# FFN second product of groups 0 to 7 as seven block products (Strassen), in a two-layer decoder trunk on one core

## The chip, the cores and the metric

One core of one Trainium2 chip. The metric is device time in microseconds (us) of one execution. The core has TensorE (PE in the profile, its weight loads PEld), VectorE (DVE), ScalarE (ACT), GpSimd (POOL) and SyncE (SP), which issues most transfers. Each engine takes its instructions in the written order and waits on semaphores.

## The reference, cut to what matters

A stream `x` of 256 tokens by 1024 goes through two layers, each a mixer (attention) and a convolutional FFN, with residual and layer norm behind each. All values are float32. The change is in the FFN:

```
def conv_ffn(x, w_in, conv_w, conv_b, w_out):      # w_in 1024 x 5632, w_out 2816 x 1024
    up, gate = split(x @ w_in, 2)
    up = depthwise causal conv of width 3 over tokens (up) + conv_b
    return (gelu(up) * gate) @ w_out
x = layer_norm(ALPHA * x + conv_ffn(x, ...))
```

## The kernel before

`yoco_trunk` writes out each engine's program by hand. Float32 precision is had with three matmuls: each operand is split into a rounded part (`hi`, by ACT, line 790) and the rest (`lo`, by DVE, line 977, as `raw - hi`), and `product` (lines 1286 to 1290) adds hi*hi, hi*lo and lo*hi into one PSUM bank of 512 columns. Weights come in chunks of 128 x 2048 elements (1 MB) into a ring of three `raw` tiles, and are split into rings of four `w_hi` and `w_lo` tiles.

The FFN works through 11 groups of 256 features. For group i:

- `in_product(i)` (line 1462): 16 products, 48 matmuls, tokens as rows, `up` and `gate` features as columns, for two halves of tokens (`st`). Each half fills one bank; two pairs of banks alternate from group 1 on (`in_banks`).
- `turn_in` (line 1206, DVE) transposes each of the two banks in 32x32 blocks into `turned`; `in_move` (line 586, SP) carries the blocks to `in_moved` (a part of the tile `kT`) with four transfers.
- `taps` (lines 897, 898, ACT), `add_taps` (lines 1226, 1229, DVE), `make_gelu` (line 910, ACT), `make_hidden` (line 1214, DVE), `make_h_hi` (line 918, ACT) and `make_h_lo` (line 1219, DVE) make the hidden features, features on partitions, in a ring of four (`HIDDEN`, held in `oT_hi`, `oT_lo`).
- `out_product` (line 1490): 8 products of 128 x 128 by 128 x 512 for the group (two halves of tokens, two halves of output columns, two halves of features), 24 matmuls, summed over all groups in the four banks `wide`. It follows three groups behind `in_product` (`second_behind`).

So PE does 72 matmuls of 512 columns in a group. POOL does almost nothing in the FFN: six weight half splits (line 731) near the layer norms and small powers (lines 754, 763). On SP's queue a group's turned blocks are moved ahead of the load six chunks later (`MOVE_AHEAD`).

Of the kernel before, what the change touches and what calls it, by code (L numbers as in the profile page):

```python
# [39 lines left out]
HIDDEN = 4  # L40
MOVE_AHEAD = 6
# [261 lines left out]
def yoco_trunk(nc, x, positions, a_w_qkv, a_w_o, w_kv_shared, b_w_q, b_w_o, b_lambda, b_subln_g,  # L303
# [14 lines left out]
    LAYER_CHUNKS = QKV_CHUNKS + WO_CHUNKS + 3 * GROUPS  # L318
# [29 lines left out]
    def second_behind(i):  # L348

        if i == GROUPS - 1:  # L350
            return [GROUPS - 4, GROUPS - 3]
        return [i - 3] if i >= 3 else []

    ffn_order = []
    for i in range(GROUPS):
        ffn_order += [(i, 0), (i, 1)] + [(n, 2) for n in second_behind(i)]
    ffn_order += [(GROUPS - 2, 2), (GROUPS - 1, 2)]

    def ffn_chunk(layer, i, which):

        return layer * LAYER_CHUNKS + QKV_CHUNKS + WO_CHUNKS + ffn_order.index((i, which))

    IN_CHUNKS = {ffn_chunk(layer, i, h) for layer in range(LAYERS) for i in range(GROUPS) for h in range(2)}

    def raw_count(c):

        return sum(32 if n in IN_CHUNKS else 16 for n in range(c % RAW_RING, c + 1, RAW_RING))

    ffn_moves_ahead = {}
    for layer in range(LAYERS):  # L370
        for i in range(GROUPS):
            ffn_moves_ahead[ffn_chunk(layer, i, 1) + MOVE_AHEAD] = (layer, i)
# [33 lines left out]
    with ExitStack() as ctx:  # L406
# [6 lines left out]

        raw = [sb(f"raw{s}", [P, CHUNK]) for s in range(RAW_RING)]
# [5 lines left out]
        qk_rows = sb("qk_rows", [P, 2 * ST * HALF])  # L420
# [3 lines left out]
        v_rows = sb("v_rows", [P, ST, D])  # L424
# [17 lines left out]
        conv = headT[0][:, 0:2, :]  # L442
# [1104 lines left out]
```

## Time and profile before

| | us |
|---|---|
| median of 3 runs | 592.69 |
| lowest, highest | 592.50, 593.11 |
| the profiled execution's own time | 593.44 |
| its span, first to last instruction | 590.9 |
| FFN of layer 0 on PE, about | 113.5 to 294.8 |
| FFN of layer 1 on PE, about | 401 to 582 |

The profile is of one execution, 0.1% above the median. The page's busy time of PE counts matmuls from start to modelled end, which overlap: the time that one adds is the distance between two starts. The time of a DVE, ACT or POOL instruction runs from its start to its end; back to back, DVE's overlap by some hundredths of a microsecond. The granted TensorE clock is 1.00 in the windows of both FFN stages.

### The profile page before, as it was taken

Reading aid. Unit: us, or ns where it says so; the run is one execution under the profiler, and the core shown is the slowest. Engines: PE = TensorE matmul, PEld = TensorE weight load, DVE = VectorE, ACT = ScalarE, POOL = GpSimd, SP = SyncE. Lnnn points to the kernel's source line nnn. Section 1 sums busy time; section 2 is a strip of 40 time slices with the busy share of each in tenths; the row PEclk is TensorE's granted clock in tenths of the full one; section 3 lists DMA queues with packets and bytes.
Section 4 is the critical chain, followed back from the end, with each engine's and each line's share of the span. In section 5 each row is a group of like instructions: output and inputs, shape, how many; then the busy total and the mean of one; then the engine's idle time right before and its main releaser. Section 6 shows DMA issues by size and latency. Waiting matters only on the chain.

```text
span 590.9 us, 7752 instructions
## 1 busy us (share of the span) xinstructions
PE 580.6 (98%) x2720; PEld 473.7 (80%) x2720; DVE 448.5 (76%) x813; ACT 335.3 (57%) x560; POOL 50.9 (9%) x84
## 2 busy tenths in 40 slices
PE   8999999999999999999999999999999999999995
PEld 6887777788888888888888888887888888888884
DVE  4889995886688777667879796778677888766656
ACT  4767584245566656554545678944556574555530
POOL 5300000400000000000120003132000000000003
PEclk9999999999999999999999999999999999999998
DMA  8997876456668798866456955442965889777511
GB/s 298 297 325 232 273 176 214 132 182 207 202 211 262 252 336 259 262 207 219 154 202 192 333 175 174 136 143 72 311 184 181 252 257 334 243 235 246 179 36 71
DMA packets 95665, 127.86 MB, mean 216 GB/s; under 512 B 13404, under 2 KB 73612, under 8 KB 95628
## 3 DMA queue, kind: packets, MB, share of 16 engines
q1 hardware_dynamic: 94188, 123.19, 65.3%
q0 software_dynamic: 1152, 4.19, 2.0%
q8 instruction: 21, 0.34, 0.2%
q14 instruction: 16, 0.13, 0.1%
q10 hardware_dynamic: 288, 0.00, 0.0%
HBM read 108.23 MB, written 1.05 MB: 185 GB/s over the span
## 4 chain that ended last, share of the span: by engine, by line
PE 95%; DVE 3%; DMA 1%; ACT 0%; issue 0%; SPq 0%; DVEq 0%
PE wide L1288 18%; PE wide L1290 17%; PE wide L1289 17%; PE score L1290 6%; PE score L1288 6%; PE score L1289 6%; PE outb L1290 3%; PE turn L1290 3%; PE outb L1288 3%; PE turn L1288 3%; PE outb L1289 3%; PE turn L1289 3%; DMA xs<-in_x 1%; DVE xT L994 1%; PE turn L1387 1%; PE outb L1413 1%
## 5 line engine op out<-in xcount | busy, mean ns | idle before, releaser
L977 DVE TENSOR_TENSOR w_lo<-raw,w_hi 128x2048 fp32r<-128x2048 f32 (+1 forms) x120 | 210.5, 1776 | 60.5 <-ACT w_hi L790 60.3
L790 ACT ACTIVATE w_hi<-raw 128x2048 fp32r<-128x2048 f32 (+1 forms) x126 | 184.2, 1488 | 92.3 <-PE wide L1290 45.5
L1288 PE MATMUL wide<-w_hi,oT_hi 128*128 128x512 f32 x240 | 95.0, 396 | 0.0
L1290 PE MATMUL wide<-w_hi,oT_lo 128*128 128x512 f32 x240 | 93.5, 390 | 0.0
L1289 PE MATMUL wide<-w_lo,oT_hi 128*128 128x512 f32 x240 | 93.5, 390 | 0.0
L1288 PE MATMUL wide<-w_hi,xT 128*128 128x512 f32 x224 | 89.9, 401 | 0.5 <-DVE xT L994 0.3
L1290 PE MATMUL wide<-w_hi,xT 128*128 128x512 f32 x224 | 87.4, 390 | 0.0
L1289 PE MATMUL wide<-w_lo,xT 128*128 128x512 f32 x224 | 87.3, 390 | 0.0
L1288 PE MATMUL score<-w_hi,xT 128*128 128x512 f32 x160 | 62.2, 389 | 0.0
L1289 PE MATMUL score<-w_lo,xT 128*128 128x512 f32 x160 | 62.2, 389 | 0.0
L1290 PE MATMUL score<-w_hi,xT 128*128 128x512 f32 x160 | 62.2, 389 | 0.0
L1290 PEld LDWEIGHTS wide<-w_hi,oT_lo 128*128 128x128 f32 x240 | 45.0, 188 | 9.5
L1288 PEld LDWEIGHTS wide<-w_hi,oT_hi 128*128 128x128 f32 x240 | 45.1, 188 | 9.1 <-issue 0.3
L1289 PEld LDWEIGHTS wide<-w_lo,oT_hi 128*128 128x128 f32 x240 | 45.1, 188 | 8.9
L1288 PEld LDWEIGHTS wide<-w_hi,xT 128*128 128x128 f32 x224 | 42.1, 188 | 11.5 <-issue 2.9
L1290 PEld LDWEIGHTS wide<-w_hi,xT 128*128 128x128 f32 x224 | 42.0, 188 | 9.0
L1289 PEld LDWEIGHTS wide<-w_lo,xT 128*128 128x128 f32 x224 | 42.1, 188 | 7.9
L897 ACT ACTIVATE kT<-kT 128x256 f32<-128x256 f32 x44 | 17.9, 406 | 51.5 <-DMA kT<-turned 51.5
L1226 DVE SCALAR_TENSOR_TENSOR qT<-kT,conv_cols,qT 128x255 f32<-128x255 f32 x44 | 21.1, 480 | 25.1 <-ACT qT L898 25.1
L1289 PEld LDWEIGHTS score<-w_lo,xT 128*128 128x128 f32 x160 | 30.0, 188 | 6.3
L1290 PEld LDWEIGHTS score<-w_hi,xT 128*128 128x128 f32 x160 | 30.0, 188 | 6.3
L1288 PEld LDWEIGHTS score<-w_hi,xT 128*128 128x128 f32 x160 | 30.0, 188 | 6.1
(160 smaller groups left out, 837.9 us busy)
## 6 DMA issues: line engine op xcount, KB each, us to landing
raw<-in_ffn_w_in SPq DMA_DIRECT2D x88, 512.0 KB, 5.4
raw<-in_ffn_w_out SPq DMA_DIRECT2D x22, 1024.0 KB, 7.6
kT<-turned SPq DMA_DIRECT2D x104, 128.0 KB, 2.8
raw<-in_a_w_qkv SPq DMA_DIRECT2D x9, 1024.0 KB, 6.8
raw<-in_w_kv_shared SPq DMA_DIRECT2D x8, 1024.0 KB, 7.0
raw<-in_a_w_o SPq DMA_DIRECT2D x4, 1024.0 KB, 6.2
raw<-in_b_w_q SPq DMA_DIRECT2D x4, 1024.0 KB, 5.1
raw<-in_b_w_o SPq DMA_DIRECT2D x4, 1024.0 KB, 5.2
```

The lines of the kernel that those rows point to most:

```text
L790: ins = nc.scalar.activation(w_hi[c % RING][:, part], raw[c % RAW_RING][:, part], ACT.Copy)
L897: nc.scalar.activation(by_quarters(up[:, tt, :]), carried(tt), ACT.Copy)
L977: ins = nc.vector.tensor_tensor(w_lo[c % RING][:, part], raw[c % RAW_RING][:, part], w_hi[c % RING][:, part].bitcast(F32), ALU.subtract)
L994: nc.vector.tensor_tensor(xT_lo[part], side[f][:, :].rearrange("p (k q) -> p k q", k=4), xT_hi[part].bitcast(F32), ALU.subtract).then_inc( ...
L1226: link(nc.vector.scalar_tensor_tensor(conv[:, tt, 1:SEQ], up[:, tt, 0:SEQ - 1], conv_cols[:, layer, FT + 2 * i + tt:FT + 2 * i + tt + 1], ...
L1288: nc.tensor.matmul(dst, a_hi, b_hi, start=start, stop=False, skip_group_check=True)
L1289: nc.tensor.matmul(dst, a_hi, b_lo, start=False, stop=False, skip_group_check=True)
L1290: return nc.tensor.matmul(dst, a_lo, b_hi, start=False, stop=stop, skip_group_check=True)
L1387: last = nc.tensor.transpose(turn_bank[:, b * P:(b + 1) * P], probs[:, slot, b * P:(b + 1) * P], ident[:, :])
L1413: nc.tensor.matmul(part[h][:, 0:SEQ], v_rows[:, 0, col:col + 64], turned_probs[:, (head + h) % 4, 0:2], start=n == 0, stop=False, skip_gro ...
```

## The change

For groups 0 to 7 (`FOLDED`) the second product, a 2 x 2 by 2 x 2 multiplication of blocks (halves of tokens, of features and of output columns), is done by Strassen's seven products instead of eight. Each is summed over the eight groups in a bank of its own: seven banks, `fold_a` (four) and `fold_b` (three). One bank, `side[3]`, is left for the first product of groups 2 to 9, so each half of `in_half` waits until DVE has transposed the half before it.

Five of the seven take sums of two blocks on each side. The sums of hidden blocks are made by DVE (`combine`), and DVE subtracts for seven `h_lo` blocks instead of four. The sums of weight blocks, five in all, are made by POOL (`fold_weights`) from the raw chunk, and POOL also makes their `lo` parts; ACT makes the `hi` parts (`fold_plain_hi`, `fold_sum_hi`, `fold_b_hi`), and DVE the `lo` part of the two blocks used as they are (`fold_plain_lo`). After the last folded product DVE adds the seven banks into `xs` with 12 instructions (`add_folded`). Group 10 has its first product with features on partitions (`in_features`), 96 matmuls of 256 columns instead of 48 of 512, and needs no transposition or move. Four half splits of the second weights of groups 8 and 9 go from DVE to POOL. Each folded group's second weights are loaded ahead of the move of its turned blocks.

```diff
-HIDDEN = 4
-MOVE_AHEAD = 6
+FOLDED = 8
...
         for i in range(GROUPS):
             loads += [("chunk", in_chunk(layer, i, h)) for h in range(2)]
             if 2 <= i < FOLDED + 2:
                 loads.append(("fold", FOLDED * layer + i - 2))
...
-        in_banks = [side[0:2], side[2:4]]
+        fold_a = ((1, wide[0]), (0, side[0]), (2, side[2]), (3, side[1]))
+        fold_b = ((6, wide[1]), (5, wide[3]), (4, wide[2]))
...
+            def fold_weights(t):
+
+                four = quadrants(t)
+                pool.wait_ge(raw_in[raw_slot("fold", t)], raw_count("fold", t))
+                if t:
+                    pool.wait_ge(sum_lo_done, t)
+                nc.gpsimd.tensor_tensor(fold_sums[0].rearrange("p (t n) -> p t n", t=2), four[:, :, 0, :], four[:, :, 1, :],
+                                        ALU.add).then_inc(sums_a_done, 1)
+                if t:
+                    pool.wait_ge(fold_b_lo_done, t)
+                nc.gpsimd.tensor_tensor(fold_sums[1][:, 0:D].rearrange("p (h n) -> p h n", h=2), four[:, 1, :, :], four[:, 0, :, :],
+                                        ALU.subtract)
+                nc.gpsimd.tensor_tensor(fold_sums[1][:, D:D + HALF], four[:, 0, 0, :], four[:, 1, 1, :],
+                                        ALU.add).then_inc(sums_b_done, 1)
+                pool.wait_ge(sum_hi_done, t + 1)
+                nc.gpsimd.tensor_tensor(fold_lo[0][:, CHUNK // 2:CHUNK], fold_sums[0], fold_hi[0][:, CHUNK // 2:CHUNK].bitcast(F32),
+                                        ALU.subtract).then_inc(sum_lo_done, 1)
+                pool.wait_ge(fold_b_hi_done, t + 1)
+                nc.gpsimd.tensor_tensor(fold_lo[1], fold_sums[1], fold_hi[1].bitcast(F32),
+                                        ALU.subtract).then_inc(fold_b_lo_done, 1)
...
+                def combine(i):
+
+                    dve.wait_ge(hidden_done, 2 * (GROUPS * layer + i) + 2)
+                    sums, tile = h_sums, hidden_tiles
+                    nc.vector.tensor_tensor(sums[:, 0:2, :], tile[:, 0:2, :], tile[:, 2:4, :], ALU.add)
+                    nc.vector.tensor_tensor(sums[:, 2:4, :], tile[:, 1:4:2, :], tile[:, 0:4:2, :], ALU.subtract)
+                    nc.vector.tensor_tensor(sums[:, 4, :], tile[:, 0, :], tile[:, 3, :], ALU.add).then_inc(combined_done, 1)
...
+                    if i > 2 or (i, st) == (2, 1):
+                        pe.wait_ge(in_turned, ST * u + st)
...
+                def in_features(which):
...
+                    for tt in range(2):
+                        into = side[3 - which][:, tt * SEQ:(tt + 1) * SEQ]
+                        for kt in range(KT):
...
+                            last = product(into, w_hi[c % RING][:, col:col + P], w_lo[c % RING][:, col:col + P],
+                                           xT_hi[:, kt, :], xT_lo[:, kt, :], kt == 0, kt == KT - 1)
...
+                def out_folded(j, half):
...
+                    for n, (tile, bank) in enumerate(fold_b if half else fold_a):
+                        if half == 0 and n == 2:
+                            pe.wait_ge(sum_lo_done, t + 1)
+                        cols = slice(n * HALF, (n + 1) * HALF)
+                        last = product(bank[:, :], hT_hi[b][:, tile, :], hT_lo[b][:, tile, :],
+                                       fold_hi[half][:, cols], fold_lo[half][:, cols], j == 0, j == FOLDED - 1)
...
-                for i in range(GROUPS):
-                    in_product(i)
-                    for n in second_behind(i):
...
+                for i in range(MOVES):
+                    for st in range(ST):
+                        in_half(i, st)
+                        if i >= 2:
+                            out_folded(i - 2, st)
+                for which in range(2):
+                    in_features(which)
```

DVE in one middle group of layer 0, before. `qT` holds the convolution, gelu and hidden features, `kT` what came by `in_move`, `oT_lo` the hidden features' `lo` part:

```order
L1206 STREAM_TRANSPOSE turned<-score 128x16x32 [waits in_carried,in_rows_done]
L977 TENSOR_TENSOR w_lo<-raw,w_hi 128x2048 [waits hi_done]
L1206 STREAM_TRANSPOSE turned<-score 128x16x32 [waits chunk_used]
L1219 TENSOR_TENSOR oT_lo<-qT,oT_hi 128x256 [waits hhi_done] x2
L977 TENSOR_TENSOR w_lo<-raw,w_hi 128x2048 [waits hi_done] x2
L1226 SCALAR_TENSOR_TENSOR qT<-kT,conv_cols,qT 128x255 [waits tap_done]
L1229 SCALAR_TENSOR_TENSOR qT<-kT,conv_cols,qT 128x254 [waits dve_step]
```

DVE there now, from the last tap of the group before to the weight splits; ahead of these rows stand one transposition and three more taps. `masked` holds the sums of hidden blocks:

```order
L1390 SCALAR_TENSOR_TENSOR qT<-qT,conv_cols 128x254 [waits dve_step]
L1335 TENSOR_TENSOR qT<-qT,kT 128x256 [waits gelu_done,hhi_done]
L1335 TENSOR_TENSOR qT<-qT,kT 128x256 [waits gelu_done]
L1345 TENSOR_TENSOR masked<-qT 128x256 [waits hidden_done]
L1346 TENSOR_TENSOR masked<-qT 128x256
L1347 TENSOR_TENSOR masked<-qT 128x128
L1354 TENSOR_TENSOR fold_lo_a<-raw,fold_hi_a 128x1024 [waits plain_hi_done]
L1362 TENSOR_TENSOR oT_lo<-masked,oT_hi 128x640 [waits hhi_done]
L1365 TENSOR_TENSOR oT_lo<-qT,oT_hi 128x256 [waits hhi_done]
L1323 STREAM_TRANSPOSE turned<-outb 128x16x32 [waits chunk_used]
L1095 TENSOR_TENSOR w_lo<-raw,w_hi 128x2048 [waits hi_done] x2
```

One full weight split left the group, three sums, a half-size split and a longer `lo` came in, and the second transposition stands behind them.

POOL from the FFN of layer 0 to the mixer of layer 1, before:

```order
L739 DMA norm_rows<-in_ln_b 128x1024
L763 TENSOR_TENSOR std_inv<-var_eps,minus_half 128x1 [waits var_done]
L731 TENSOR_TENSOR w_lo<-raw,w_hi 128x1024 [waits hi_done,norm_x_done] x2
L763 TENSOR_TENSOR std_inv<-var_eps,minus_half 128x1 [waits var_done]
L754 TENSOR_TENSOR rms_inv<-mean_sq,minus_half 128x2 [waits mean_sq_done] x4
```

POOL now, the last of eight folded groups and what follows it (`kT` and `spare` hold the sums of weight blocks):

```order
L796 TENSOR_TENSOR kT<-raw 128x1024 [waits sum_lo_done,raw_in1]
L800 TENSOR_TENSOR spare<-raw 128x1024 [waits fold_b_lo_done]
L802 TENSOR_TENSOR spare<-raw 128x512
L805 TENSOR_TENSOR fold_lo_a<-kT,fold_hi_a 128x1024 [waits sum_hi_done]
L808 TENSOR_TENSOR fold_lo_b<-spare,fold_hi_b 128x1536 [waits fold_b_hi_done]
L779 TENSOR_TENSOR w_lo<-raw,w_hi 128x1024 [waits hi_done] x4
L836 TENSOR_TENSOR std_inv<-var_eps,minus_half 128x1 [waits var_done]
```

The five long instructions at the head of these rows stand eight times in each layer's FFN, where POOL had none.

## Rows read from the trace of the kernel before

**Rows 1.** The page's first part: busy time, share, instructions of each engine.

```profile
PE 580.6 (98%) x2720; PEld 473.7 (80%) x2720; DVE 448.5 (76%) x813; ACT 335.3 (57%) x560; POOL 50.9 (9%) x84
```

**Rows 2.** Waits of PE: engine, line, releaser: us, times, longest.

```profile
PE wide L1309 <- DVE oT_hi L1037: 1.5, 1, 1.5
PE turn L1301 <- DVE xs L1034: 1.0, 2, 0.5
```

**Rows 3.** Timeline of PE, group 1, first product: start us, us, what.

```profile
133.22 0.39 PE L1290 MATMUL score<-w_hi,xT 128*128 128x512 f32 x1
...
133.90 0.39 PE L1290 MATMUL score<-w_hi,xT 128*128 128x512 f32 x1
```

**Rows 4.** Groups by line and shape: busy us, mean ns, idle before.

```profile
L977 DVE TENSOR_TENSOR w_lo<-raw,w_hi 128x2048 fp32r<-128x2048 f32 x63 | 143.3, 2284 | 46.1 <-ACT w_hi L790 45.9
L790 ACT ACTIVATE w_hi<-raw 128x2048 fp32r<-128x2048 f32 x64 | 122.2, 1912 | 67.2 <-PE wide L1290 28.2 <-DMA raw<-in_ffn_w_in 24.4 <-PE outb L1290 8.1
...
L977 DVE TENSOR_TENSOR w_lo<-raw,w_hi 128x1024 fp32r<-128x1024 f32 x57 | 67.2, 1215 | 14.4 <-ACT w_hi L790 14.4
...
L790 ACT ACTIVATE w_hi<-raw 128x1024 fp32r<-128x1024 f32 x62 | 62.0, 1051 | 25.1 <-PE wide L1290 17.3 <-DMA raw<-in_a_w_qkv 7.8
...
L898 ACT ACTIVATE qT<-kT,conv_cols 128x256 f32<-128x256 f32 x44 | 25.8, 587 | 0.0
L1229 DVE SCALAR_TENSOR_TENSOR qT<-kT,conv_cols,qT 128x254 f32<-128x254 f32 x44 | 21.3, 483 | 1.6
...
L1214 DVE TENSOR_TENSOR qT<-qT,kT 128x256 f32<-128x256 f32 x44 | 18.4, 422 | 3.9 <-ACT qT L910 1.7
...
L897 ACT ACTIVATE kT<-kT 128x256 f32<-128x256 f32 x44 | 17.9, 406 | 51.5 <-DMA kT<-turned 51.5
...
L731 POOL TENSOR_TENSOR w_lo<-raw,w_hi 128x1024 fp32r<-128x1024 f32 x6 | 14.4, 2409 | 56.4 <-DVE w_lo L977 51.1 <-DVE xs L1034 5.3
L1206 DVE STREAM_TRANSPOSE turned<-score 128x512 f32<-128x512 f32 x20 | 14.2, 710 | 2.7 <-PE score L1290 2.7
...
L994 DVE TENSOR_TENSOR xT<-score,xT 128x512 fp32r<-128x512 f32 x8 | 5.5, 688 | 7.9 <-ACT xT L800 7.9
...
L769 POOL TENSOR_TENSOR xs<-xs,norm_rows 128x512 f32<-128x512 f32 x2 | 2.5, 1277 | 1.1 <-ACT xs L948 1.1
```

**Rows 5.** Windows: busy time of each engine inside layer 0's FFN.

```profile
core 0: us, PE busy (x) PEld busy (x) DVE busy (x) ACT busy (x) POOL busy (x), PEclk, DMA share, GB/s
125.00:285.00 160.00, 160.00 (x707) 132.48 (x707) 116.58 (x144) 90.20 (x120) 1.13 (x2) 1.00 0.77 246
```

**Rows 6.** Timeline of DVE and POOL where a long DVE instruction runs.

```profile
359.51 1.22 DVE L977 TENSOR_TENSOR w_lo<-raw,w_hi 128x1024 fp32r<-128x1024 f32 x1
359.68 1.61 POOL L754 TENSOR_TENSOR rms_inv<-mean_sq,minus_half 128x2 f32<-128x2 f32 x1 [59.64 <-DVE mean_sq L1165]
```

**Rows 7.** The same two engines, 5 us later, beside a shorter one.

```profile
364.31 0.48 DVE L1181 SCALAR_TENSOR_TENSOR oT_lo<-turn,sub_gain,oT_hi 128x256 fp32r<-128x256 f32 x1
...
364.48 0.69 POOL L754 TENSOR_TENSOR rms_inv<-mean_sq,minus_half 128x2 f32<-128x2 f32 x1 [1.64 <-DVE mean_sq L1165]
```

**Rows 8.** Timeline of POOL while DVE is idle.

```profile
11.49 0.26 POOL L695 TENSOR_SCALAR turns<-turns 128x16 f32<-128x16 f32 x1
```

**Rows 9.** Timeline of POOL, the same operation while DVE splits weights.

```profile
15.40 0.53 POOL L703 TENSOR_SCALAR turns<-turns 128x16 f32<-128x16 f32 x1
```

**Rows 10.** Timeline of DVE: one split where a POOL instruction ends, one elsewhere.

```profile
14.50 0.71 DVE L1043 TENSOR_TENSOR w_lo<-raw,w_hi 128x512 fp32r<-128x512 f32 x1
...
16.34 0.68 DVE L1043 TENSOR_TENSOR w_lo<-raw,w_hi 128x512 fp32r<-128x512 f32 x1
```

**Rows 11.** Timeline of PE: four transpositions of 128 columns, then a product.

```profile
118.21 0.63 PE L1301 MATMUL turn<-ident,xs 128*128 128x128 f32 x4 [0.50 <-DVE xs L1034]
118.59 0.48 PE L1288 MATMUL wide<-w_hi,xT 128*128 128x512 f32 x1
```

**Rows 12.** Timeline of PE: its first six matmuls of 512 columns.

```profile
1.45 2.93 PE L1309 MATMUL wide<-oT_hi 128*128 128x512 f32 x6 [1.45 <-DVE oT_hi L1037]
```

More of the change, by code:

```diff
@@ L325, in yoco_trunk @@
         POOL_SPLITS[2 * layer, 0] = ([(c + 1, 0)], [(c + 1, 1)])
+        POOL_SPLITS[2 * layer, 1] = ([], [(c + 2 * GROUPS + n, half) for n in range(2) for half in range(2)])
         c = (layer + 1) * LAYER_CHUNKS
@@ L328, in yoco_trunk @@
             POOL_SPLITS[2 * layer + 1, 0] = ([], [(c + 1, 1), (c + 2, 0)])
-    POOL_PARTS = [part for n in range(2 * LAYERS) for st in range(ST) for parts in POOL_SPLITS.get((n, st), ([], [])) for part in parts]
+    for n in range(2 * LAYERS):
+        for st in range(ST):
+            for parts in POOL_SPLITS.get((n, st), ([], [])):
+                POOL_PARTS += parts
     POOL_CHUNKS = sorted({c for c, _ in POOL_PARTS})
@@ L938, in _ @@
+                    if 1 <= i <= FOLDED:
+                        fold_b_hi(i - 1)
+                    if i < GROUPS - 1:
+                        split_hi(in_chunk(layer, i, 1) + RING)
+                make_h_hi(GROUPS - 1)
+                for c in (base + LAYER_CHUNKS, base + LAYER_CHUNKS + 1):
+                    for half in range(2):
+                        split_hi(c, half)
                 if layer + 1 < LAYERS:
@@ L1222, in add_taps, with add_folded @@
+                def add_folded(adds):
+                    for st, half, bank, op, after in adds:
+                        part = xs[:, st, half * HALF:(half + 1) * HALF]
+                        if after:
+                            dve.wait_ge(folded_added, 12 * layer + after)
+                        nc.vector.scalar_tensor_tensor(part, part, 1.0 if after else ALPHA, bank[:, :], ALU.mult,
+                                                       op).then_inc(folded_added, 1)
                 def add_taps(i):
@@ L1260, in _ @@
+                    split_lo(in_chunk(layer, i, 0) + RING)
+                    if i < MOVES:
+                        split_lo(in_chunk(layer, i, 1) + RING)
+                    else:
+                        make_h_lo(i)
+                        for half in range(2):
+                            split_lo(base + LAYER_CHUNKS, half)
+                        if layer + 1 < LAYERS:
+                            split_shared_lo()
                     if (layer, i) == (0, 0):
@@ L1266, in _ @@
                 n, c = 2 * layer + 1, base + LAYER_CHUNKS
+                dve.wait_ge(folded_added, 12 * (layer + 1))
                 residual(n, 0, 0)
@@ L1503, in out_product @@
-                    return last
-                for i in range(GROUPS):
-                    in_product(i)
-                    for n in second_behind(i):
-                        for st in range(ST):
-                            for half in range(2):
-                                last = out_product(n, st, half)
-                        last.then_inc(chunk_used, 1)
+                        last = product(wide[2 * st + half][:, :], hT_hi[b][:, at + 2 * tt + st, :], hT_lo[b][:, at + 2 * tt + st, :],
+                                       w_hi[c % RING][:, cols], w_lo[c % RING][:, cols], i == FOLDED and tt == 0,
+                                       i == GROUPS - 1 and tt == 1)
```

391 lines of the change are left out of this document (252 added, 139 removed).

## Prediction, made before the changed kernel was run

> **What bounds the kernel now.** I read the page's first part, then what PE waits for, then its timeline inside the FFN. PE is busy 98% of the span [rows 1], its waits for other engines are five, 3.2 us in sum, the longest two 1.5 and 0.5 [rows 2], and in the FFN the next matmul starts 0.68 us after the third before it, from 133.22 to 133.90 [rows 3]: 0.2267 us for each 512 columns. The busy mean of one (0.39) is no price, since neighbours overlap. So PE bounds both FFN stages, and a group costs 72 x 0.2267 = 16.3 us. In a window of 160 us inside the FFN, DVE is busy 116.6 us, ACT 90, POOL 1.1 [rows 5]. DVE has 27% to spare, and POOL looks free. Whether it is free is the question of this case.
>
> **PE's part.** Each folded group has seven products instead of eight, so three matmuls fewer: 8 groups x 2 layers x 3 = 48, and 48 x 0.2267 = **-10.9 us**. A folded group is 69 x 0.2267 = 15.64 us of PE. Group 10 swaps 48 matmuls of 512 columns for 96 of 256. No row has such a matmul with a 128-column weight load. Bounds: four transpositions of 128 columns take 0.38 us up to the next start [rows 11], 0.095 each, which gives 96 x 0.095 - 10.9 = -1.8 us a layer; a matmul that costs the full 0.2267 whatever its columns gives +10.9. Half of 0.2267 is 0.113; a straight line through 0.095 at 128 and 0.2267 at 512 gives 0.139. I take 0.12, near the half: 96 x 0.12 - 10.9 = +0.6 a layer, **+1.3 us**. PE alone would then give 593.4 - 10.9 + 1.3 = 583.8 for the profiled execution.
>
> **DVE's part.** A group's work in order, durations from [rows 4]: two transpositions of 0.71; four taps of 0.48 (1.93); two multiplications of 0.42 (0.84); three sums of hidden blocks (0.42, 0.42, and for 128 columns between nothing and 0.42, say 0.29: 1.13); the half-size split 1.22; the `lo` part of 640 columns, between 0.69 at 512 and 1.22 at 1024, say 0.82, and 0.40 for 256 by the multiplications' 0.42; two weight splits of 2.28 (4.57). That is 10.9 us without the transpositions, 12.3 with them, against PE's 15.64. The twelve adds of the banks (0.69 each, one operand in PSUM) lie beside group 10's two first products, 11.5 us of PE, of which the second waits for five of them only; I cost them at nothing. If that cover were gone they would cost at most 8 us a layer.
>
> **POOL's part.** Five instructions a folded group: sums of 1024, 1024 and 512 columns, `lo` parts of 1024 and 1536. The split of 1024 takes 2.41 us, one of 512 takes 1.28 [rows 4], 1536 by proportion 3.61. Sum 2.41 + 2.41 + 1.28 + 2.41 + 3.61 = 12.1 us a group. Alone this too fits under 15.64.
>
> **Where they meet.** DVE's 10.9 us are all instructions with both tensor inputs in SBUF, and so are POOL's 12.1. Before, POOL's long instructions lie beside DVE work with an operand in PSUM, and are 2.41 us without a spread. The small ones tell more. A POOL power on two columns takes 0.69 us beside a DVE instruction that reads PSUM [rows 7], and 1.61 us when a DVE weight split starts 0.17 us ahead of it: it ends 0.56 us after the split does [rows 6]. An operation on 16 columns takes 0.26 us while DVE is idle [rows 8] and 0.53 us while DVE runs weight splits [rows 9]. So POOL waits until DVE's instruction is through. In the other direction a DVE split of 512 columns takes 0.71 us where a POOL instruction of 16 columns ends inside it, and 0.68 elsewhere [rows 10]: DVE seems held for the short moment that POOL needs. That no POOL instruction of 2.4 us stands against a DVE one with two SBUF inputs leaves the size open. Bounds for a folded group: 15.64 us (PE's, if a running POOL instruction never holds DVE and waits little itself) and 10.9 + 12.1 = 23.0 us (each excludes the other in full). I take 23.0, because both directions are seen at small size and POOL's long instructions read two operands all the time.
>
> The Trainium skill ("SBUF — State Buffer", "Who interferes with whom") says that a DVE instruction with two SBUF inputs contends with a GpSimd instruction that reads SBUF, and that the later of the two is blocked for the whole of the other. By that rule the bound is the upper one; the rows above agree as to POOL's waiting, and no row here shows the rule for a long POOL instruction.
>
> **Does the order allow 23.0?** Lay out one period from the second transposition of a group (0.0), when ACT has just made the sums' `hi` part. POOL `lo` 0 to 2.4, beside the transposition; DVE split 2.4 to 4.7; POOL's long `lo` 4.7 to 8.3; DVE split 8.3 to 10.6; transposition of the next half 10.6 to 11.3 beside POOL's first sum, 10.6 to 13.0; then taps, with POOL's second sum (13.5 to 15.9) and third (16.4 to 17.7) between them, to 18.6; multiplications 19.5, block sums 20.6, half split 21.8, `lo` parts 23.0, next transposition. The shared resource is never idle, and the period closes at 23.0. Small idle moments would add; DVE rows that overlap by some hundredths would take away; I leave both out.
>
> PE has one bank for the first product, so it waits for each transposition. Without POOL it gives DVE 7.5 us and 8.2 us between them and loses nothing; here the intervals are 10.6 and 12.4 us, so PE idles 7.4 us a period.
>
> **Sum.** For a layer, seven full periods (groups 1 to 7): 7 x (23.0 - 15.64) = 51.7. Behind the last one the interval to group 9's first transposition is 10.6 instead of 7.5: 3.1. In group 1, where PE has only 10.9 us of work, DVE's 10.9 and POOL's first sums of 6.1 meet; POOL can do these earlier or not, 0 to 6.1, I take 3. Together 57.8 us a layer, **+115.6 us**. SP's load of the second weights ahead of the moves costs nothing: the load's last condition (POOL's third sum, DVE's half split, at 21.8) precedes the move's (the transposition's end). If it came later, the move (four transfers, which ACT's taps need) would be late by as much, a few microseconds a group at worst, inside the range. ACT has, from [rows 4], two full `hi` splits (3.8), two halves (2.1), one of 1536 (1.5), taps (2.0), and two gelus and two `hi` parts of hidden blocks at about 0.4 to 0.7 each (1.9): 11.3 us a group, below PE's 15.64.
>
> 583.8 + 115.6 = 699.4 us for the profiled execution; the median of the runs lies 0.75 lower: **699 us**.
>
> **Rivals.**
> 1. *The engines do not hold each other.* Then PE bounds at 15.64 a group and the time is 583.8 - 0.8 = **583 us**, faster. For it: DVE's 12.3 and POOL's 12.1 both fit under PE, and of the 7.5 and 8.2 us between transpositions DVE needs 5.3 (0.71 + 4.57) and 7.0 (0.71 + 1.93 + 0.84 + 1.13 + 1.22 + 1.22). Against it: rows 6 and 9 beside rows 7 and 8. It decides if DVE's splits keep 2.28 us while POOL's instructions run.
> 2. *Only POOL waits, DVE goes on beside a running POOL instruction.* Each of POOL's five starts can lose the rest of a DVE instruction, on average half of 1 us, at most 2.28. POOL's group becomes 12.1 + 2.5 to 12.1 + 5 = 14.6 to 17.1 us, up to 1.5 over PE, 16 times: 583 to **607 us**, on both sides of no change. For it: only small instructions are seen to hold DVE. Against it: [rows 10].
> 3. *TensorE's clock falls in PE's new gaps* of 2 to 5 us, which the trace before does not have. At its start six matmuls take 2.93 us [rows 12], 0.46 us from start to start, twice the 0.2267. If all PE work of a period ran so, 31.3 us would exceed 23.0, and 14 periods would add 14 x 8.3 = 116 us: **815 us**. Against it: PE's halves are 5.4 us long, and at half speed each takes 10.9, still within the 10.6 to 12.4 us that DVE leaves less the short second products; only a clock that never recovers decides it. A partial fall is hidden.
>
> The Trainium skill ("TensorE: Matmul & The Clock Gate", "What's actually happening") says that an idle array is throttled to half clock and activity releases it. That would show as granted clock 0.5 in PE's gaps; by it alone some of rival 3 happens, hidden under DVE. No row of the FFN before has a gap that tests it.
>
> **Chances.** Forecast (the exclusion, between 640 and 760) 0.74; rival 1 0.14; rival 2 0.08, spread 0.03 faster, 0.02 same, 0.03 slower; rival 3 0.04. Faster by over 0.2% 0.17, within 0.2% (about what a measurement of this kernel can tell) 0.02, slower 0.81. The range goes down into rival 2's span, past any partial exclusion (each microsecond less in the period takes 14 to 16 us off), and up to a period with 4.4 us of idle in it (14 x 4.4 = 61): 590 to 760. Outside it are rivals 1 and 3, 0.18, and the low end of rival 2.
>
> **What would show it.** Right: in the FFN after, DVE's w_lo splits of 2048 columns have a mean well over 2.28 us and POOL's 1024-column sums over 2.41 (waiting inside the instruction) or gaps ahead of them; DVE and POOL busy sum to more than the stretch; PE waits for `turned`, about 7 us a group in groups 2 to 9; seven to eight periods of 23 us; PE's span outside the FFN is unchanged. Wrong: periods of 15.6 to 16.3 us and PE at 98%. The 256-column matmuls' starts lie 0.12 us apart in group 10; at 0.227 the sum is short by 20 us.

## The result, and the profile after

The changed kernel takes **694.53 us** (median of 4 runs, 692.70 to 694.73) against 592.76 in the same session: 1.171 times as long, 95% interval 1.1689 to 1.173. That is 4.5 us below the forecast of 699. The profiled execution took 694.53 us, with a span of 692.7.

The page's first part, to be held against [rows 1] (busy time, share of the span, instructions):

```profile
PE 608.2 (88%) x2768; PEld 487.1 (70%) x2768; DVE 586.2 (85%) x877; ACT 363.0 (52%) x592; POOL 311.1 (45%) x172
```

No engine is full. DVE has 64 instructions more than before and 138 us more of busy time; POOL has 260 us more. What PE waits for (engine, line, releaser: us in sum, times, longest), where [rows 2] had two small waits:

```profile
PE outb L1456 <- DVE turned L1323: 58.7, 21, 6.6
PE wide L1456 <- DVE oT_lo L1371: 9.4, 3, 4.5
PE wide L1456 <- DVE turned L1323: 6.3, 2, 3.5
```

The groups of instructions by line and shape (busy us, mean ns of one), the answers to [rows 4]:

```profile
L1095 DVE TENSOR_TENSOR w_lo<-raw,w_hi 128x2048 fp32r<-128x2048 f32 x43 | 151.0, 3515 | 29.3 <-ACT w_hi L864 29.3
L1095 DVE TENSOR_TENSOR w_lo<-raw,w_hi 128x1024 fp32r<-128x1024 f32 x57 | 67.2, 1214 | 13.9 <-ACT w_hi L864 13.9
L1387 DVE SCALAR_TENSOR_TENSOR qT<-qT,conv_cols 128x255 f32<-128x255 f32 x44 | 63.6, 1446 | 11.0 <-ACT qT L980 11.0
L808 POOL TENSOR_TENSOR fold_lo_b<-spare,fold_hi_b 128x1536 fp32r<-128x1536 f32 x16 | 75.4, 4710 | 12.7 <-ACT fold_hi_b L1032 12.7
L796 POOL TENSOR_TENSOR kT<-raw 128x1024 f32<-128x1024 f32 x16 | 64.6, 4038 | 32.7 <-DMA raw<-in_ffn_w_out 32.6
```

The DVE split of 2048 columns, 2284 ns before, has a mean of 3515. The one of 1024 columns, used outside the FFN, is unchanged. A tap of 0.48 us takes 1.45. POOL's sum of 1024 columns has a mean of 4.04 us against 2.41 for a like one. So the time is lost **inside** instructions. One period of the FFN shows it one by one. First DVE (start us, us), from one second transposition to the next:

```profile
208.26 0.71 DVE L1323 STREAM_TRANSPOSE turned<-outb 128x512 f32<-128x512 f32 x1
209.99 2.77 DVE L1095 TENSOR_TENSOR w_lo<-raw,w_hi 128x2048 fp32r<-128x2048 f32 x1 [1.03 <-ACT w_hi L864]
213.16 5.09 DVE L1095 TENSOR_TENSOR w_lo<-raw,w_hi 128x2048 fp32r<-128x2048 f32 x1 [0.40 <-ACT w_hi L864]
218.18 0.70 DVE L1323 STREAM_TRANSPOSE turned<-outb 128x512 f32<-128x512 f32 x1
218.81 1.98 DVE L1387 SCALAR_TENSOR_TENSOR qT<-qT,conv_cols 128x255 f32<-128x255 f32 x1
220.83 2.50 DVE L1390 SCALAR_TENSOR_TENSOR qT<-qT,conv_cols 128x254 f32<-128x254 f32 x1
223.25 1.51 DVE L1387 SCALAR_TENSOR_TENSOR qT<-qT,conv_cols 128x255 f32<-128x255 f32 x1
...
229.31 0.70 DVE L1323 STREAM_TRANSPOSE turned<-outb 128x512 f32<-128x512 f32 x1
```

Then POOL in the same stretch:

```profile
208.23 2.38 POOL L805 TENSOR_TENSOR fold_lo_a<-kT,fold_hi_a 128x1024 fp32r<-128x1024 f32 x1 [4.80 <-ACT fold_hi_a L1024]
211.41 4.70 POOL L808 TENSOR_TENSOR fold_lo_b<-spare,fold_hi_b 128x1536 fp32r<-128x1536 f32 x1 [0.79 <-ACT fold_hi_b L1032]
...
217.19 3.31 POOL L796 TENSOR_TENSOR kT<-raw 128x1024 f32<-128x1024 f32 x1
220.47 2.57 POOL L800 TENSOR_TENSOR spare<-raw 128x1024 f32<-128x1024 f32 x1
223.00 1.48 POOL L802 TENSOR_TENSOR spare<-raw 128x512 f32<-128x512 f32 x1
```

Read the two together. POOL's first instruction runs beside the transposition and takes its plain 2.38 us. The DVE split that starts at 209.99 ends at 212.76, 2.15 us after POOL's end at 210.61. POOL's next starts at 211.41, inside that split, and ends at 216.11, 3.35 us after the split. The second split starts at 213.16, inside POOL's, and ends at 218.25, 2.14 us after it. So each finishes a little less than its own duration after the other's end, and the same holds for the taps: the one of 2.50 us ends 0.29 us after POOL's 2.57 do. The transpositions keep their 0.70 even with POOL beside them. The Trainium skill ("SBUF — State Buffer", "Who interferes with whom") says that such contention is an exclusive lock, and that the order of issue decides who blocks; this trace agrees for POOL's long instructions, up to the 0.1 to 0.2 us by which each handover is shorter than the waiting instruction's own duration.

The distance between second transpositions of a group is 21.06 us in the mean of the seven periods of layer 0: 187.17 to 208.26 and 208.26 to 229.31 are two of them.

### The profile page after: what moved, and what is told of

It reads as the page before. It is cut to its first block, busy times and chain, and to the rows that moved or that the text cites. A ratio compares the mean times of both kernels' runs of the same rounds, so it can differ in the third digit from the quotient of the medians.

```text
span 692.7 us, 8052 instructions
## 1 busy us (share of the span) xinstructions
PE 608.2 (88%) x2768; PEld 487.1 (70%) x2768; DVE 586.2 (85%) x877; ACT 363.0 (52%) x592; POOL 311.1 (45%) x172
## 4 chain that ended last, share of the span: by engine, by line
PE 44%; DVE 26%; ACT 13%; issue 12%; DMA 3%; SPq 1%; DVEq 0%; ACTq 0%
PE wide L1456 10%; PE wide L1458 10%; PE wide L1457 10%; DVE qT L1387 8%; DVE qT L1390 7%; ACT w_hi L864 6%; PE outb L1456 3%; PE outb L1457 3%; PE outb L1458 2%; ACT fold_hi_b L1032 2%; DVE turned L1323 2%; DVE w_lo L1095 2%; ACT fold_hi_a L1024 2%; DMA raw<-in_ffn_w_out 2%; DMA kT<-turned 2%
## 5 line engine op out<-in xcount | busy, mean ns | idle before, releaser
L1095 DVE TENSOR_TENSOR w_lo<-raw,w_hi 128x1024 fp32r<-128x1024 f32 (+1 forms) x100 | 218.2, 2204 | 43.2 <-ACT w_hi L864 43.2
L864 ACT ACTIVATE w_hi<-raw 128x1024 fp32r<-128x1024 f32 (+1 forms) x110 | 153.3, 1422 | 60.9 <-PE wide L1458 27.1
L1456 PE MATMUL outb<-w_hi,xT 128*128 128x512 f32 x256 | 112.2, 438 | 58.7 <-DVE turned L1323 58.7
L1456 PEld LDWEIGHTS outb<-w_hi,xT 128*128 128x128 f32 x256 | 53.4, 208 | 81.2 <-DVE turned L1323 69.9
L1457 PE MATMUL outb<-w_lo,xT 128*128 128x512 f32 x256 | 108.7, 425 | 0.0
L1458 PE MATMUL outb<-w_hi,xT 128*128 128x512 f32 x256 | 107.8, 421 | 0.0
L992 ACT ACTIVATE qT<-qT 128x256 f32<-128x256 f32 x44 | 18.4, 418 | 149.3 <-DVE qT L1390 149.3
L808 POOL TENSOR_TENSOR fold_lo_b<-spare,fold_hi_b 128x1536 fp32r<-128x1536 f32 x16 | 75.4, 4710 | 12.7 <-ACT fold_hi_b L1032 12.7
L796 POOL TENSOR_TENSOR kT<-raw 128x1024 f32<-128x1024 f32 x16 | 64.6, 4038 | 32.7 <-DMA raw<-in_ffn_w_out 32.6
L1387 DVE SCALAR_TENSOR_TENSOR qT<-qT,conv_cols 128x255 f32<-128x255 f32 x44 | 63.6, 1446 | 11.0 <-ACT qT L980 11.0
L1458 PEld LDWEIGHTS outb<-w_hi,xT 128*128 128x128 f32 x256 | 53.5, 209 | 12.5
L1457 PEld LDWEIGHTS outb<-w_lo,xT 128*128 128x128 f32 x256 | 53.4, 209 | 11.0
L1390 DVE SCALAR_TENSOR_TENSOR qT<-qT,conv_cols 128x254 f32<-128x254 f32 x44 | 55.3, 1256 | 1.6
```

Source lines behind the costliest of these rows:

```text
L796: nc.gpsimd.tensor_tensor(fold_sums[0].rearrange("p (t n) -> p t n", t=2), four[:, :, 0, :], four[:, :, 1, :], ALU.add).then_inc(sums_a_do ...
L808: nc.gpsimd.tensor_tensor(fold_lo[1], fold_sums[1], fold_hi[1].bitcast(F32), ALU.subtract).then_inc(fold_b_lo_done, 1)
L864: ins = nc.scalar.activation(w_hi[c % RING][:, part], raw[raw_slot("chunk", c)][:, part], ACT.Copy)
L992: nc.scalar.activation(gelu[:, tt, :], conv[:, tt, :], ACT.Gelu_apprx_tanh).then_inc(gelu_done, 1)
L1095: ins = nc.vector.tensor_tensor(w_lo[c % RING][:, part], raw[raw_slot("chunk", c)][:, part], w_hi[c % RING][:, part].bitcast(F32), ALU.sub ...
L1387: link(nc.vector.scalar_tensor_tensor(conv[:, tt, 1:SEQ], up[:, tt, 0:SEQ - 1], conv_cols[:, layer, FT + 2 * i + tt:FT + 2 * i + tt + 1], ...
```

## The experiments

Ratios are against runs of the kernel before on the same chip, whose medians lie between 592.99 and 593.07 us. Each experiment has a short name, `b1` to `b3` on the kernel before and `e1` to `e8` on the changed kernel.

**`b1`: does a POOL that reads cost time in the kernel before?** Nothing of the change is in it; each FFN group gets ten subtractions of 512 columns on POOL.

```diff
+                for _ in range(10):
+                    twice = ident[:, :].unsqueeze(1).broadcast_to([P, 4, P])
+                    probe_link(nc.gpsimd.tensor_tensor(probe_out.rearrange("p (a b) -> p a b", a=4), twice, twice, ALU.subtract))
```

> The kernel before, with added work on POOL alone that nothing waits for: in each of the 22 FFN groups ten subtractions of 512 columns with both inputs in SBUF (12.8 us at 1.28 each), started by the group's first transposition. PE, DVE, ACT and SP are as before. Exclusion theory: DVE's 10.4 us a group with two SBUF inputs (three splits of 2.28, taps 1.93, multiplications 0.84, lo parts 0.80) and POOL's 12.8 cannot overlap: 21 to 23 us a group instead of 16.3, the time 692 to 740 us, and DVE's splits of 2048 columns last about 3.5 us in the mean. Rival, only POOL waits or nobody does: PE stays at 16.3 us a group, 592.8 us, splits at 2.28.

Measured: 666.85 us, ratio 1.1246 (1.1223 to 1.1268). The direction holds, but the expectation is missed at its low end by 25 us. POOL's added instructions and DVE's splits, by line and shape:

```profile
L756 POOL TENSOR_TENSOR masked<-ident 128x512 f32<-128x512 f32 x220 | 347.0, 1577 | 52.9 <-DVE turned L1225 37.3
L996 DVE TENSOR_TENSOR w_lo<-raw,w_hi 128x2048 fp32r<-128x2048 f32 x63 | 172.0, 2750 | 3.3 <-ACT w_hi L809 3.3
```

A split goes from 2284 to 2750 ns, not to some 3500: a POOL instruction of 512 columns is short, and a split waits for the rest of one and no more. The added work was also priced too high. The median of these 220 subtractions is 1.10 us and the shortest takes 1.04, where 1.28 was taken, so ten of them and DVE's 10.4 us make about 20.8 us a group and not 23; measured are 16.3 + 73.8 / 22 = 19.7. That the rest is the shorter handovers seen above was not shown.

**`b2`: and a POOL that only writes?** In place of the ten subtractions, twenty fills of the same tile.

```diff
-                for _ in range(10):
+                for _ in range(20):
+                    probe_link(nc.gpsimd.memset(probe_out, 0.0))
```

> The same kernel with the added POOL work as twenty fills of 512 columns a group in place of ten subtractions: POOL is busy about as long, and writes SBUF, but reads nothing from it. Exclusion theory, as an exclusion of reads: 592.8 us within 0.3%, splits at 2.28 us. If what holds DVE is POOL's use of SBUF in any way, reads or writes, or its load of semaphores: as slow as the kernel with the subtractions.

Measured: 592.97 us, ratio 1.0001 (0.999 to 1.0011). POOL's 117 us of busy time in a window of 160 us of the FFN touch nothing; PE stays full. The window (PE, PEld, DVE, ACT, POOL busy, granted clock), which answers to [rows 5]:

```profile
125.00:285.00 160.00, 160.00 (x707) 132.48 (x707) 116.72 (x144) 90.29 (x120) 117.22 (x222) 1.00 0.77 246
```

**`b3`: and a POOL that reads one input?** The ten subtractions become ten copies.

```diff
+                    probe_link(nc.gpsimd.tensor_copy(probe_out.rearrange("p (a b) -> p a b", a=4), twice))
```

> The kernel before with ten extra POOL copies of 128 x 512 in each FFN group: the run with subtractions again, but each with one input read and not two. Subtractions cost 73.8 us (666.85), fills that read nothing cost nothing (592.97). Theory a (VectorE and POOL hold each other wherever both have two inputs to read, and a copy has one): within 2 us of 593. Theory b (any read by POOL does it): 620 to 665, by POOL's busy time in proportion, and the low splits of 128 x 2048 longer than their 2284 ns.

Measured: 596.49 us, ratio 1.0057 (1.0042 to 1.0073). The time is far below theory b's range and above theory a's. The same window, and DVE's splits:

```profile
125.00:285.00 160.00, 158.41 (x699) 130.84 (x698) 137.25 (x140) 87.60 (x116) 130.60 (x112) 1.00 0.76 243
L996 DVE TENSOR_TENSOR w_lo<-raw,w_hi 128x2048 fp32r<-128x2048 f32 x63 | 158.1, 2524 | 21.5 <-ACT w_hi L809 21.5
```

Copies do slow DVE: 137.25 us busy against 116.72, and 2524 ns a split against 2284. How they do it stands in the timeline. Two copies and two DVE splits, one by one:

```profile
202.19 2.55 POOL L756 COPY masked<-ident 128x512 f32<-128x512 f32 x1
204.80 2.56 POOL L756 COPY masked<-ident 128x512 f32<-128x512 f32 x1
201.57 2.70 DVE L996 TENSOR_TENSOR w_lo<-raw,w_hi 128x2048 fp32r<-128x2048 f32 x1
204.19 2.69 DVE L996 TENSOR_TENSOR w_lo<-raw,w_hi 128x2048 fp32r<-128x2048 f32 x1
```

The first copy ends at 204.74, 0.47 us after the first split (204.27), and the second split ends at 206.88, 2.14 us after that copy. The second copy ends 0.48 us after the second split. That is the same exclusion in both directions as in the changed kernel, with the same 2.14. So theory b had the mechanism and only the price wrong: a copy takes 0.69 us where nothing holds it (0.61 the shortest), not 1.28, and for most of its 2.55 us it stands waiting. Ten copies of 0.69 and DVE's 10.4 us make 17.3 us a group by the durations, and 15.1 with the 0.47 us that a copy adds behind a split; both are near PE's 16.3, and the measured group is (596.49 - 593.07) / 22 = 0.16 us longer.

**`e1`: the change with POOL's reading taken out.** Each of POOL's five instructions of a folded group becomes two fills of its output, so the sums of the second weights and their `lo` parts are left out.

```diff
-                nc.gpsimd.tensor_tensor(fold_sums[0].rearrange("p (t n) -> p t n", t=2), four[:, :, 0, :], four[:, :, 1, :],
-                                        ALU.add).then_inc(sums_a_done, 1)
+                nc.gpsimd.memset(tile, 0.0).then_inc(fill_step, 1)
+                pool.wait_ge(fill_step, filled[0])
+                nc.gpsimd.memset(tile, 0.0).then_inc(done, 1)
...
```

> The changed kernel, with POOL's five instructions of each folded group replaced by fills of the same tiles, each done twice to last about as long; the order and the waits of all engines stay. The sums of weight blocks and their lo parts are therefore left out of the result. Exclusion theory: DVE's instructions go back to their own length, the period falls from 21.06 us to PE's 15.64 to 16.3, and the time to 584 to 600 us. Rival, the time comes from the chain of handovers between POOL, ACT and DVE or from the single bank for the first product: it stays near 694 us.

Measured: 610.41 us, ratio 1.0299 (1.0282 to 1.0317). The splits are back at 2276 ns and the period is 15.64 us, exactly PE's 69 x 0.2267. So the 84 us between this and the changed kernel go with POOL's reading. (The fills of a group take some 9.6 us and not 12.1, by their rows of 0.95, 0.53 and 1.38 us, so POOL's chain is also 2.5 us shorter here; `e4` below keeps the sums, on the other engine.) But it is slower than the kernel before by 17, above the expected range: something else costs time, and none of it lies in the periods of 15.64 us. PE's waits, of which the prediction had only 3 us a layer, for the start:

```profile
PE wide L1463 <- DVE oT_lo L1378: 8.9, 2, 4.5
PE outb L1463 <- DVE turned L1330: 8.1, 2, 4.1
```

One wait of each kind lies in each layer: for `turned` at the start of the FFN (behind PE's matmul of 144.9 us in layer 0) and for `oT_lo` in its tail (behind that of 287.8).

**`e4`: POOL's five instructions on DVE instead.**

```diff
-            def fold_weights(t):
+                def fold_weight_sums(t):
...
-                nc.gpsimd.tensor_tensor(fold_lo[1], fold_sums[1], fold_hi[1].bitcast(F32),
-                                        ALU.subtract).then_inc(fold_b_lo_done, 1)
+                    nc.vector.tensor_tensor(fold_lo[1], fold_sums[1], fold_hi[1].bitcast(F32),
+                                            ALU.subtract).then_inc(fold_b_lo_done, 1)
```

> The changed kernel with POOL's five instructions of each folded group moved to DVE, which needs 6.1 us for them (1.22, 1.22, 0.69, 1.22 and about 1.75). Exclusion theory: a folded group is then bound by DVE alone, 12.3 + 6.1 = 18.4 us instead of 21.06, so more work on the busier engine makes it faster: 14 periods x 2.7 = 37 us less, about 657 us (645 to 670). Rival, DVE is simply the overloaded engine and POOL relieves it: 6.1 us more in each period, 780 us.

Measured: 632.8 us, ratio 1.0672 (1.0656 to 1.0688). All the work is still done, and it takes 62 us less than with POOL's help. DVE does the subtraction of 1536 columns in 1.75 us, POOL needs 3.35 after DVE is through, so work that excludes DVE's is best done by DVE. The period is 17.23 us; I had expected 18.4 from the durations. They hold some 0.06 us each that the next instruction overlaps, over about 20 instructions. The time lies 12 us below the expected range. 14 periods give 14 x (21.06 - 17.23) = 53.6 of the 62 us; the expectation had no term for the start and the tail, where in layer 0 group 1's second transposition comes at 142.59 and not 145.15, and the interval behind the last period is 7.82 and not 9.95.

**`e3`: the move ahead of the load again**, the second part of the change undone alone:

```diff
-            entry = ("chunk", in_chunk(layer, i + 3, 0) if i < FOLDED else out_chunk(layer, i))
+            entry = ("fold", FOLDED * layer + i) if i < FOLDED else ("chunk", out_chunk(layer, i))
```

> The changed kernel with the second part of the change undone alone: a group's turned-block transfers go ahead of the load of its second weights on SP's queue again. Theory (the load has slack either way, the pattern of VectorE and POOL sets the period of 21.06 us): 694 to 697. Rival (the load then lands after POOL is ready for its first sum, 8.9 us after the transposition, and the chain of sums is pushed back by some 1 to 2 us in each of 14 periods): 700 to 715.

Measured: 695.03 us, ratio 1.1716 (1.1697 to 1.1735). The period stays, 21.05 to 21.09 us from the second of layer 0 on. This part of the change is worth nothing that these runs can tell.

**`e2`: the half splits of the second weights of groups 8 and 9 back on DVE.**

```diff
-        POOL_SPLITS[2 * layer, 1] = ([], [(c + 2 * GROUPS + n, half) for n in range(2) for half in range(2)])
+        POOL_SPLITS[2 * layer, 1] = ([], [])
```

> The changed kernel with the splits of out chunks 8 and 9 taken back from POOL and given to DVE (four splits of half a chunk, of both layers). In the trace of the changed kernel POOL's long split of such a half (4.94 us, L779) holds the taps of DVE and ACT behind it in the tail of each FFN. Theory (the lost time lies in the half-period pattern, the start and the tail, and in the tail mostly on the late load): 0 to 8 us less than the changed kernel, 687 to 695. Rival (POOL's splits are what makes the tail late): 10 us less or more, under 685.

Measured: 694.64 us, ratio 1.1705 (1.1683 to 1.1726). No gain. PE's waits show an exchange: the 9.4 us for `oT_lo` become 3.9 for it and 5.9 for the adds of the seven banks (`xs`, line 1380).

**`e6`: the loads of groups 8 and 9 ahead of these groups' moves.** In the tail of the changed kernel ACT, DVE and POOL stand so, from the last transposition on:

```profile
318.32 1.91 ACT L864 ACTIVATE w_hi<-raw 128x2048 fp32r<-128x2048 f32 x1 [10.02 <-DMA raw<-in_ffn_w_out]
320.45 0.59 ACT L980 ACTIVATE qT<-kT,conv_cols 128x256 f32<-128x256 f32 x1
321.07 1.93 DVE L1387 SCALAR_TENSOR_TENSOR qT<-qT,conv_cols 128x255 f32<-128x255 f32 x1 [3.96 <-ACT qT L980]
323.03 2.50 DVE L1390 SCALAR_TENSOR_TENSOR qT<-qT,conv_cols 128x254 f32<-128x254 f32 x1
320.31 4.94 POOL L779 TENSOR_TENSOR w_lo<-raw,w_hi 128x1024 fp32r<-128x1024 f32 x2 [7.17 <-ACT w_hi L864]
```

ACT stands idle for 10.02 us for group 9's second weights, and its taps stand behind that split. The load is issued behind the move of group 9, whose condition is the last transposition (309.05). So the taps start at 320.45, and POOL's split, released by the same load, then holds DVE's taps.

```diff
-            entry = ("chunk", in_chunk(layer, i + 3, 0) if i < FOLDED else out_chunk(layer, i))
+            entry = ("chunk", in_chunk(layer, i + 3, 0) if i < FOLDED else out_chunk(layer, i + 1))
```

> The changed kernel with the loads of the second weights of groups 8 and 9 put ahead of the moves of those groups' turned blocks on SP's queue. In the trace ScalarE stands idle for 10.02 us for the load of group 9 in the tail, and TensorE waits 9.4 us for what is queued behind. Theory: about 5 us less in each layer, 684 (680 to 689). Rival (the tail is late by the engines' own work, not by the load): within 2 us of the changed kernel, 692 to 696.

Measured: **679.64 us**, ratio 1.1458 (1.1438 to 1.1478): 14.9 us less than the changed kernel, 7.4 a layer, half as much again as expected. The wait for `oT_lo` was 9.4 us, 4.7 a layer; the other 2.7 are matmuls at the lower clock behind it, read in the next section. All of this wait is gone, the others are nearly as they were (58.8 us against 58.7, and 5.9 against 6.3), and ACT's split no longer waits for the load:

```profile
308.56 1.92 ACT L864 ACTIVATE w_hi<-raw 128x2048 fp32r<-128x2048 f32 x1 [0.80 <-PE outb L1458]
316.48 1.14 DVE L1387 SCALAR_TENSOR_TENSOR qT<-qT,conv_cols 128x255 f32<-128x255 f32 x1
...
PE outb L1456 <- DVE turned L1323: 58.8, 21, 6.6
```

**`e8`: the same with POOL only filling**, `e1`'s and `e6`'s edits together (sums and their `lo` parts left out):

> The changed kernel in which POOL's five instructions of a Strassen group are replaced by fills that read nothing (the sums of the second weights and their low parts are left out, so their values are not those of the product), and the loads of groups 8 and 9 go ahead of those groups' moves. The first of the two alone gave 610.4 us with a period of 15.64 us, that is TensorE's own. Theory (what stands above TensorE's 583.8 us is a late load in the tail and a wait for the first transposed blocks at the start of each FFN): about 10 us less than 610.4, 600 (597 to 604), with TensorE's wait for the low parts of the hidden blocks gone. Rival (POOL's long splits make the tail late): 606 to 610.

Measured: 597.1 us, ratio 1.0066 (1.0045 to 1.0087), 13.3 us less than `e1`. The tail's wait is gone, as in the run above; what is left are waits for `turned`:

```profile
PE outb L1463 <- DVE turned L1330: 8.1, 2, 4.1
PE wide L1463 <- DVE turned L1330: 1.2, 2, 0.7
```

Both lie at the start of each FFN. There DVE's program has group 0's sums, half split and `lo` parts (from 139.01) ahead of the transposition of group 1's second half, and these wait for group 0's moved blocks. Behind it stand two weight splits, and then the transposition of group 2's first half. DVE's timeline from there, in this run:

```profile
142.10 0.71 DVE L1330 STREAM_TRANSPOSE turned<-wide 128x512 f32<-128x512 f32 x1
143.84 2.29 DVE L1102 TENSOR_TENSOR w_lo<-raw,w_hi 128x2048 fp32r<-128x2048 f32 x1 [1.03 <-ACT w_hi L871]
147.02 2.29 DVE L1102 TENSOR_TENSOR w_lo<-raw,w_hi 128x2048 fp32r<-128x2048 f32 x1 [0.89 <-ACT w_hi L871]
149.23 0.71 DVE L1330 STREAM_TRANSPOSE turned<-outb 128x512 f32<-128x512 f32 x1
```

And in the kernel before, the same two splits, with the transposition of group 1's second half between them:

```profile
139.72 2.29 DVE L977 TENSOR_TENSOR w_lo<-raw,w_hi 128x2048 fp32r<-128x2048 f32 x1
141.93 0.71 DVE L1206 STREAM_TRANSPOSE turned<-score 128x512 f32<-128x512 f32 x1
...
143.20 2.28 DVE L977 TENSOR_TENSOR w_lo<-raw,w_hi 128x2048 fp32r<-128x2048 f32 x1
```

That transposition comes at the same time, but the splits start 4.1 and 3.8 us later. They wait for their `hi` parts, which ACT starts at 141.91 and 145.09 (before at 137.79 and 140.21), behind the `hi` parts of group 0's sums. The last row of this run is the transposition of group 2's first half, which PE had finished before it went on to the matmuls from 142.96; it frees the only bank PE has left for first products. PE's last start is at 145.55, the next at 149.99, when the transposition is done.

**`e7`: all of it on DVE, with the earlier loads**: the five instructions and the half splits on DVE, loads as in `e6`.

> The changed kernel with POOL's five instructions of a Strassen group on VectorE, the half splits of chunks 8 and 9 on VectorE too, and the loads of groups 8 and 9 ahead of those groups' moves. The first of these three alone gave 632.8. Theory (the edges are the late load and POOL's long splits, the gains add): 632.8 less 10 less 3 = 620 (615 to 626). Rival (with the sums on VectorE the tail is bound by VectorE itself): 629 to 633.

Measured: 624.77 us, ratio 1.0531 (1.0514 to 1.0548), 8.0 below `e4` where I had summed 13. PE still waits 3.7 us for `oT_lo`: with everything on DVE the tail is late there. It is the fastest version that does the whole work as seven products, and still 32 us slower than the kernel before. `e8` says why no placing of the sums alone would win: even with sums that cost nothing, what the starts of the two FFNs lose (14 us) is more than the 10 us that seven products save PE.

## Why the prediction was right, and where its terms were off

**What bounds the kernel, and PE's part: right.** With no one in the way a folded group takes 15.64 us (`e1`, `e8`), the number of the sum. In `in_features` 48 matmuls of 256 columns go from 310.89 to 316.52 us, 0.120 from start to start: the 0.12 taken between the bounds. So 583.8 for PE alone stood, 583.0 against the median. `e8` bears it out: its profiled execution took 596.62 us, and without 9.3 of waits and an estimated 2 x 1.7 of slower matmuls (below) that is 583.9.

**The exclusion: right, and it decided the sign.** Rival 1 falls with `b1` and `e1`, rival 2 with the split of 5.09 us: POOL's running instruction does hold DVE. That DVE is simply overloaded falls with `e4`, where it does POOL's work too and the time drops by 62 us.

**The period: mis-sized, 21.06 and not 23.0.** The interval behind a second transposition was put at 10.6 and is 9.92 to 9.97 in layer 0 from group 2 on; the other was put at 12.4 and is 11.11 to 11.14. The step that failed is the one that took the rows' durations as the time for which one engine excludes the other and left overlaps out. In the rows above a DVE split ends 2.14 us after POOL's instruction, not 2.28, and a tap 0.29 after it, not 0.48; DVE's neighbours overlap by 0.06 to 0.09 (207.19 + 0.82 against a next start at 207.92). Some eight handovers of 0.13 to 0.2 and nine such overlaps come to about 2 us, which is an estimate from these rows. The term was put at 51.7 a layer and is 7 x (21.06 - 15.64) = 37.9.

**Into group 9: 2.4 us where 3.1 was taken.** 9.95 less 7.5.

**The start of the FFN: 3 taken, about 8 measured.** The 3 stood for POOL's part, and that held: group 1's second transposition comes at 145.15 us in the changed kernel and at 142.10 in `e8`, where POOL only fills, 3.05 us earlier. What I did not see is the order: group 0's sums and the `hi` and `lo` parts made of them stand ahead of the weight splits and so of group 2's first transposition. This is a term that was put at nothing. With the clock behind it, it costs (597.1 - 583.0) / 2 = 7 us a layer with no exclusion at all; without the 1.7 us of the clock (below), which DVE hides in the changed kernel, some 5.3 are left, an estimate.

**The tail: nothing taken, 7.4 measured.** The sum of the seven banks was costed at nothing, and that held: no wait for it is in the changed kernel, it only shows once DVE has the half splits too (`e2`). What failed is the step on SP's order, which looked at groups 0 to 7, where it is worth nothing (`e3`), and not at the same table's entries for groups 8 and 9.

The sum with measured terms: 37.9 + 2.4 + 7.4 + 8.0 = 55.7 us a layer, and 583.0 + 111.4 = 694.4, against 694.53. The 8.0 is what the other terms leave, not a reading of its own; the 3.05 and the estimated 5.3 of the start come to 8.4. That the forecast came within 4.5 us is luck, since its terms' errors cancelled: 29 us too much from period and interval (2 x (51.7 + 3.1 - 37.9 - 2.4)), 25 too little from start and tail (2 x (7.4 + 8.0 - 3)).

**Rival 3, the clock: a partial fall, hidden in the periods and not in the tail.** The windows of two periods (PE busy, PEld, DVE, ACT, POOL, granted clock):

```profile
145.00:155.00 10.00, 4.58 (x12) 3.15 (x12) 8.57 (x4) 6.74 (x8) 9.08 (x3) 0.77 0.79 262
155.00:166.00 11.00, 10.02 (x33) 7.74 (x33) 10.75 (x14) 3.79 (x7) 6.26 (x3) 0.75 0.30 98
166.00:176.00 10.00, 8.50 (x36) 6.68 (x36) 8.58 (x4) 6.69 (x7) 9.15 (x3) 1.00 0.80 262
176.00:187.00 11.00, 7.82 (x33) 6.12 (x33) 10.75 (x14) 3.70 (x7) 6.34 (x3) 1.00 0.30 95
```

PE starts nothing for 5.7 us from 150.1 on. Behind that the mean granted clock is 0.75, so a part of the stretch ran at the lower of the two levels (1.2 GHz) and the rest at the higher (2.4 GHz), and PE is busy 10.02 of 11 us; at 1.00 the same 33 matmuls take 7.82. DVE's work beside them is the same 10.75 us in both. The transpositions come 20.94 us apart in the first period and 21.08 in the second, so there the slower PE costs nothing. The Trainium skill ("TensorE: Matmul & The Clock Gate", "What's actually happening") says that an idle array is throttled to half clock; this trace agrees for this gap. Not every gap has a slower stretch behind it: PE stops for 3.75 us from 205.3 and for 3.72 us from 247.4, and the rows of the two half periods that follow show 0.66 and 1.00. Why was not settled.

```profile
208.26:218.18 9.92, 9.16 (x28) 7.29 (x29) 8.49 (x5) 6.58 (x7) 9.11 (x5) 0.66 0.84 291
250.40:260.36 9.96, 8.45 (x36) 6.68 (x36) 8.54 (x4) 6.60 (x7) 9.17 (x3) 1.00 0.79 263
```

In the tail nothing hides it, since there PE itself sets the time again. PE before and behind the wait for `oT_lo`, in the changed kernel:

```profile
331.03 0.39 PE L1458 MATMUL wide<-w_hi,oT_lo 128*128 128x512 f32 x1
335.94 0.77 PE L1456 MATMUL wide<-w_hi,oT_hi 128*128 128x512 f32 x1 [4.52 <-DVE oT_lo L1371]
...
341.57 0.39 PE L1457 MATMUL wide<-w_lo,oT_hi 128*128 128x512 f32 x1
```

The 13 matmuls that start from 335.94 on take 5.63 us, most of them 0.43 from start to start, where 13 x 0.2267 = 2.95 are needed: 2.7 us lost. With layer 0's waits for `oT_lo`, 4.52 and 0.39, that makes 7.6, the 7.4 that `e6` took off a layer. In `e8` 11 matmuls from 149.99 to 154.21 take 4.22 us instead of 2.49, 1.7 lost behind the wait at the FFN's start. So "a partial fall is hidden" held for the periods only: a wait of 4 to 5 us where PE bounds cost about half as much again in slower matmuls. In the periods the slower matmuls take the place of waiting, which is in the main why PE's waits sum to 74.4 us and not to the 111 us that the time lies above PE's own; the mean granted clock of the span is 0.949, before it was 0.997.

## What to carry to other kernels

GpSimd is no spare VectorE for additions and subtractions of two SBUF tensors: while one runs, a VectorE instruction with two SBUF inputs cannot, so the two engines' times must be added, and since GpSimd is the slower the work is better left on VectorE. When such work is moved, add both engines' two-input time in a period and compare the sum, not the larger, with what TensorE needs. And where a repeated pattern is changed, lay out the first and the last round too, with every queue's table of order: here 31 of the 111 us above TensorE's own time lay there, and one entry of a table gave back 15. A wait of TensorE in such a place can cost more than itself, so look at the granted clock behind it.

## What of the hardware was not expected

Fills by GpSimd that write 232 us in all cost VectorE nothing (2285 ns a split, before 2284). Copies by GpSimd, with one input, exclude VectorE's two-input instructions just as subtractions do, and cost less only because a copy of 512 columns is short, 0.69 us: in a window of 160 us VectorE's work took 20.5 us more, and of the 130.6 us that 112 copies were busy some 53 are waiting, by 0.69 us each (an estimate). The two-input instructions' handover between the engines is shorter than the recorded durations say by 0.13 to 0.2 us each. And VectorE's transpositions (0.70 us) are not lengthened by GpSimd's two-input instructions, nor, by the 2.38 us of the one at 208.23, the other way round.
